# A decoder trunk in split precision on one core: first stage stepped by contraction tile, new orders on VectorE and ScalarE

## The reference

```python
def mixer_block(x, ...):
    h = rmsnorm(x, g_mix)
    za, zb, zc, zg = split(h @ w_in)
    ya = chunked_spatial_gating(gelu(za), ...) @ w_branch_a      # layernorm of v, masked 128x128 mix
    yb = short_gated_conv(zb, b_conv) @ w_branch_b
    yc = multiscale_pool(zc, c_wg, c_scale) @ w_branch_c
    gates = sigmoid(zg.reshape(nb, s, 3, D) + b_gate)
    return x + (gates[0] * ya + gates[1] * yb + gates[2] * yc) @ w_o

def cross_attention(x, mem, g_x, g_m, w_q, w_kv, w_o):           # 4 heads of 256
    q = rmsnorm(x, g_x) @ w_q
    k, v = split(rmsnorm(mem, g_m) @ w_kv)
    return x + softmax(q k^T * 256**-0.5) v @ w_o

def swiglu_ffn(x, g, w_in, w_out):                               # hidden 2816
    gate, up = split(rmsnorm(x, g) @ w_in)
    return x + (silu(gate) * up) @ w_out

# reference: mixer_block, cross_attention, swiglu_ffn, then rmsnorm(x, g_final)
```

## Time and profile before

| | us |
|---|---|
| median of 3 runs | 920.62 (920.34 to 920.63) |
| profiled execution | 920.04 |
| its span | 918.3 |
| TensorE busy | 900.6 (98%) |
| VectorE busy | 516.3 (56%) |
| ScalarE busy | 346.9 (38%) |
| mean granted TensorE clock | 0.995 |

### The profile page before, as it was taken

The page is one execution under the profiler, slowest core; times in us unless marked ns, Lnnn a source line. Parts: engine busy times, 40 slices in busy tenths (PEclk is TensorE's granted clock), DMA queues, the critical chain, the costliest instruction groups (busy, mean ns, idle before and its releaser), DMA issues.

```text
span 918.3 us, 12058 instructions
## 1 busy us (share of the span) xinstructions
PE 900.6 (98%) x4880; PEld 783.3 (85%) x4880; DVE 516.3 (56%) x600; ACT 346.9 (38%) x472; POOL 54.9 (6%) x59
## 2 busy tenths in 40 slices
PE   8999999999999999999999999989999999999997
PEld 6988888888888888888888888879999999888886
DVE  4576446683234245365456475988888887422333
ACT  5546322342222223232234332545545544323222
POOL 0101000000000000025100053000000000000000
PEclk9999999999999999999999999989999999999999
DMA  9842231322222222222121122222223223322212
GB/s 343 335 168 98 102 103 57 127 92 92 92 91 92 91 91 91 97 93 112 69 89 46 47 92 92 92 83 101 91 97 131 91 91 117 135 92 91 92 47 91
DMA packets 15040, 97.52 MB, mean 106 GB/s; under 512 B 1696, under 2 KB 1824, under 8 KB 4000
## 3 DMA queue, kind: packets, MB, share of 16 engines
q1 hardware_dynamic: 13968, 94.38, 28.3%
q0 software_dynamic: 464, 1.57, 0.6%
q10 hardware_dynamic: 576, 1.12, 0.4%
HBM read 94.97 MB, written 2.10 MB: 106 GB/s over the span
## 4 chain that ended last, share of the span: by engine, by line
PE 88%; DVE 6%; ACT 2%; DMA 1%; issue 1%; ACTq 0%; DVEq 0%; POOLq 0%; POOL 0%
PE psum L1253 29%; PE psum L1255 29%; PE psum L1254 29%; DVE wl L750 1%; DMA memr<-mem 1%; DVE tl L750 1%; DVE hn L1100 1%; DVE hl L753 0%; ACT th L368 0%; PE psum L1477 0%; PE psum L1303 0%; ACT pr L581 0%; PE psum L1601 0%; DVE xs L826 0%; DVE sm L1025 0%
## 5 line engine op out<-in xcount | busy, mean ns | idle before, releaser
L750 DVE TENSOR_TENSOR wl<-raw,wh 128x2048 fp32r<-128x2048 f32 (+1 forms) x56 | 116.8, 2094 | 145.3 <-ACT wh L368 145.2
L1253 PE MATMUL psum<-hh,wh 128*128 128x512 f32 x384 | 149.7, 390 | 0.0
L1255 PE MATMUL psum<-hh,wl 128*128 128x512 f32 x384 | 149.4, 389 | 0.0
L1254 PE MATMUL psum<-hl,wh 128*128 128x512 f32 x384 | 149.4, 389 | 0.0
L1253 PE MATMUL psum<-th,w7h 128*128 128x256 f32 x504 | 143.9, 285 | 5.0 <-DVE hid L1117 4.4
L1254 PE MATMUL psum<-tl,w7h 128*128 128x256 f32 x504 | 143.6, 285 | 0.0
L1255 PE MATMUL psum<-th,w7l 128*128 128x256 f32 x504 | 143.5, 285 | 0.0
L368 ACT ACTIVATE wh<-raw 128x2048 fp32r<-128x2048 f32 (+1 forms) x56 | 96.1, 1726 | 57.8 <-PE psum L1255 57.8
L1253 PEld LDWEIGHTS psum<-th,w7h 128*128 128x128 f32 x504 | 97.8, 194 | 5.7 <-DVE hid L1117 4.8
L1254 PEld LDWEIGHTS psum<-tl,w7h 128*128 128x128 f32 x504 | 97.8, 194 | 0.0
L1255 PEld LDWEIGHTS psum<-th,w7l 128*128 128x128 f32 x504 | 97.7, 194 | 0.0
(11 more groups left out here) (225 smaller groups left out, 1603.9 us busy)
## 6 DMA issues: line engine op xcount, KB each, us to landing
raw<-weights SPq DMA_DIRECT2D x79, 1024.0 KB, 4.8
vraw<-weights SPq DMA_DIRECT2D x3, 1024.0 KB, 13.7
xt<-xt SPq DMA_DIRECT2D x1, 2048.0 KB, 17.5
X<-x SPq DMA_DIRECT2D x2, 1024.0 KB, 28.2
out<-outb SPq DMA_DIRECT2D x8, 256.0 KB, 2.0
memt<-memt SPq DMA_DIRECT2D x1, 1024.0 KB, 23.4
vraw<-weights SPq DMA_DIRECT2D x2, 256.0 KB, 5.2
memr<-mem ACTq DMA_DIRECT2D x2, 256.0 KB, 7.9
```

Source lines behind the costliest of these rows:

```text
L750: return V.tensor_tensor(dst, v, f32(hi), ALU.subtract)
L1253: nc.tensor.matmul(dst, lh, rh, start=start, stop=False, **kw)
L1254: nc.tensor.matmul(dst, lh, rl, start=False, stop=False, **kw)
L1255: return nc.tensor.matmul(dst, ll, rh, start=False, stop=stop, **kw)
```

## The change

It touches six places.

1. Panels 0 and 1 of v land in pieces of 1, 1, 2, 2, 2 contraction tiles, and ScalarE and VectorE work in steps of one contraction tile: mem tile, then 512 columns of weights. The semaphores of the first eight steps are named by `of_piece`.
2. The warm-up products use `ones` alone, which POOL now writes first.
3. ScalarE and VectorE take the input's tiles in an order of their own ahead of and between the key panels.
4. The third normalization's column sums and spread stand inside tiles of the filler: ahead of contraction tile 6 of tile 0, and ahead of tile 4 of tile 1.
5. Filler 2's scaling stands between the last operand quarters, its silu ahead of the first block panel's rounding, its product behind the plain blocks. In the last seven-product panel the rounding of the weights and of `hid` are apart.
6. The tail: VectorE multiplies each half by g_final before the row factor is there; ScalarE applies the factor to the left half and issues its store.

```diff
-V_PIECES = ((0, 512), (512, 1024), (1024, 2048))
+V_PIECES = ((0, 1), (1, 2), (2, 4), (4, 6), (6, 8))
+        def of_piece(k, piece, panel):
+            return (panel, k // 4 + 1) if k % 4 == 3 else (piece, k + 1 - k // 4)
@@ gpsimd
+            nc.gpsimd.memset(ones[:], 1.0).then_inc(const_ready, 1)
             nc.gpsimd.memset(cst[:], -0.5).then_inc(const_ready, 1)
             chain(nc.gpsimd.memset(ident[:], 0.0))
-            nc.gpsimd.memset(ones[:], 1.0).then_inc(const_ready, 1)
@@ scalar
+            for k in range(KT):
+                for i, (a, b) in enumerate(MEM_PIECES):
+                    if k == a:
+                        act.wait_ge(mem_here[i], 16)
+                mem_hi(k)
+                for i, (a, b) in enumerate(V_PIECES):
+                    if k == a:
+                        act.wait_ge(v_piece[i], 16)
+                cs = slice(k % 4 * S, (k % 4 + 1) * S)
+                copy(wh[:, k // 4, cs], vraw[:, k // 4, cs]).then_inc(of_piece(k, piece_hi, hi_ready)[0], 1)
...
             h_hi(0)
+            h_hi(1)
             split_hi_halves(K0 + 2)
+            h_hi(2)
             k_hi(0)
-            h_hi(1)
+            h_hi(3)
             split_hi_halves(K0 + 3)
...
+            filler_silu(2)
             wh_blocks("plain", 0, FI0 + NF - 1, None)
             wh_blocks("s13", 0, None, 1)
             wh_blocks("s24", 0, None, 1)
             wh_blocks("corner", 0, None, None)
-            filler_silu(2)
...
-            act_window(NS - 1, 1, None, more=False, early=lambda: fo_hi(0))
+            act_window(NS - 1, 1, None, more=False, early=(lambda: fo_weights_hi(0), lambda: fo_hid_hi(0)))
...
+            def left_out(t):
+                act.wait_ge(f_rstd, t + 1)
+                act.wait_ge(f_gained, t + 1)
+                copy(outb[:, t, 0:S], outb[:, t, 0:S], scale=small(FR + t)).then_inc(f_left, 1)
+                act.wait_ge(f_left, t + 1)
+                act.dma_start(out[t * P:(t + 1) * P, 0:S], outb[:, t, 0:S]).then_inc(stored, 16)
...
+                    if half == 0 and t:
+                        left_out(t - 1)
+            left_out(TT - 1)
@@ vector
+            for k in range(KT):
+                mem_lo(k)
+                dve.wait_ge(*of_piece(k, piece_hi, hi_ready))
+                cs = slice(k % 4 * S, (k % 4 + 1) * S)
+                lo(wl[:, k // 4, cs], vraw[:, k // 4, cs], wh[:, k // 4, cs]).then_inc(of_piece(k, piece_lo, lo_ready)[0], 1)
...
             filler_product(1)
+            filler_scaled(2, 0)
             quarter_lo(5, high_banks)
+            filler_scaled(2, 1)
             dve.wait_ge(t_ready, 4)
             quarter_lo(6, low_banks)
...
             wl_plain(0, 0)
+            filler_product(2)
             wl_s13(0, 0)
-            filler_scaled(2, 0)
-            filler_scaled(2, 1)
             wl_s24(0, 0)
             wl_corner(0, 0)
-            filler_product(2)
...
+                left, right = bank[(4 + 2 * t) % 8], bank[(5 + 2 * t) % 8]
+                dve.wait_ge(f_sq, 2 * t + 1)
+                chain(V.tensor_scalar(small(FV + t), small(FS + 2 * t), 1.0 / D, EPS, ALU.mult, ALU.add))
+                V.tensor_tensor(outb[:, t, 0:S], left[:], gf[:, 0:S], ALU.mult).then_inc(f_gained, 1)
                 dve.wait_ge(f_sq, 2 * t + 2)
+                V.scalar_tensor_tensor(out=small(FV + t), in0=small(FS + 2 * t + 1), scalar=1.0 / D, in1=small(FV + t),
+                                       op0=ALU.mult, op1=ALU.add).then_inc(f_var, 1)
+                chain(V.tensor_tensor(outb[:, t, S:D], right[:], gf[:, S:D], ALU.mult))
                 dve.wait_ge(f_rstd, t + 1)
+                V.tensor_scalar(outb[:, t, S:D], outb[:, t, S:D], small(FR + t), None, ALU.mult).then_inc(f_out, 1)
@@ tensor
-            pe.wait_ge(const_ready, 3)
+            pe.wait_ge(const_ready, 1)
             for _ in range(WARM):
-                nc.tensor.matmul(bank[0][:, 0:P], ident[:], ones[:], start=True, stop=True)
+                nc.tensor.matmul(bank[0][:, 0:P], ones[:], ones[:], start=True, stop=True)
             v_half(0)
             v_half(1)
+            pe.wait_ge(const_ready, 3)
...
                     ins = fm_tile(bank[2 * (i % 2) + t], n % SLOTS, t, lambda k: hfh[:, k, :], lambda k: hfl[:, k, :],
-                                  ready=(hl_ready, 2 * KT) if i == 0 else None)
+                                  ready=(hl_ready, 2 * KT) if i == 0 else None,
+                                  between=((6, sum_x3), (4, spread_x3))[t] if i == 0 else None)
```

More of the change, by code:

```diff
@@ L200, in build @@
         mem_here = [sem(f"mem_here{i}") for i in range(3)]
-        v_piece = [sem(f"v_piece{i}") for i in range(3)]
-        v_panel = [sem(f"v_panel{i}") for i in range(4)]
+        v_piece = [sem(f"v_piece{i}") for i in range(5)]
+        v_panel = [sem(f"v_panel{i}") for i in range(2)]
         x_here = [sem(f"x_here{i}") for i in range(2)]
@@ L291, in _ @@
             for t in range(TT):
-                for half in range(2):
-                    sp.wait_ge(f_out, 2 * t + half + 1)
-                    cs = slice(half * S, (half + 1) * S)
-                    sp.dma_start(out[t * P:(t + 1) * P, cs], outb[:, t, cs]).then_inc(stored, 16)
+                sp.wait_ge(f_out, t + 1)
+                sp.dma_start(out[t * P:(t + 1) * P, S:D], outb[:, t, S:D]).then_inc(stored, 16)
             sp.wait_ge(stored, 16 * 2 * TT)
@@ L677, in act_window @@
                 if early:
-                    early()
+                    early[0]()
                 if more:
@@ L1255, in mm3, with fm_tile @@
                 return nc.tensor.matmul(dst, ll, rh, start=False, stop=stop, **kw)
-            def fm_tile(dst, slot, t, rh, rl, ks=range(KT), first=0, ready=None, free=None):
+            def fm_tile(dst, slot, t, rh, rl, ks=range(KT), first=0, ready=None, free=None, between=None):
                 for k in ks:
+                    if between and k == between[0]:
+                        between[1]()
                     if ready:
@@ L1315, in v_half @@
                         pe.wait_ge(meml_ready, k + 1)
-                    if half == 0 and k == 0:
-                        pe.wait_ge(piece_lo, 1)
-                    elif k % 4 == (1 if half == 0 and k < 4 else 0):
-                        pe.wait_ge(half_lo, n + 1)
+                        pe.wait_ge(*of_piece(k, piece_lo, lo_ready))
+                    elif k % 4 == 0:
+                        pe.wait_ge(half_lo, n - 1)
                     elif k % 4 == 2:
@@ L1527, in _, with sum_x3, spread_x3 @@
             out_part(3, range(8), True)
+            def sum_x3():
+                pe.wait_ge(res_acc, 2)
+                pe.wait_ge(exp_ready, TT * HEADS)
+                sum_columns(bank[4], acc2, TT).then_inc(res_sums, 1)
+            def spread_x3():
+                pe.wait_ge(res_rstd, 2)
+                spread(bank[4], GR, TT).then_inc(res_spread, 1)
             def filler(i):
```

112 lines of the change are left out of this document (37 added, 75 removed).

## The result

The changed kernel takes **911.34 us** (median of 4 runs, 911.21 to 911.57); the kernel before took 920.62 beside it (4 runs). The ratio is 0.9899, 95% interval 0.9882 to 0.9916. The profiled execution took 911.21 us, its span is 909.5 us; before, these were 920.04 and 918.3. The forecast was 910.2 us, range 908.6 to 912.6.

A forecast was written before the change was run, and what follows sets the result against it. TensorE was taken as the bound (88% of the chain), so gains lie only in its waits, slow clock and tail. 0.6 + 1.9 + 0 + 6.6 + 0.8 + 0.5 = 10.4 us gave 909.6 profiled, 910.2 us median, range 908.6 to 912.6.

The forecast's parts named there:

- Part 1: First stage: one-tile steps end half 0 1.5 us earlier, most given back; 0.6 us stays, bounds 0 and 1.5.
- Part 2: Keys and first v panel: the new x order removes two TensorE waits, 1.9 us, bounds 0.8 and 2.1.
- Part 5: Last seven-product panel: snapshots no longer behind the rounding of hid, idle gap goes, 0.8 us, bounds 0 and 0.8.
- Part 3: Third normalization: earlier sums and spread move VectorE's copy 2.8 us earlier; TensorE itself gains nothing.
- Part 4: Entry to seven-product panels: wait removed (4.5 us) and clock stays up (2.1 us), 6.6 us; bounds 4.5 and 6.8.
- what is next late: Second panel behind the entry: snapshot behind ScalarE's second rounding there at 605.5, wanted at 605.8, so no wait.
- Part 6: Tail: last square 0.45 us late, but shorter steps put both issues at 915.3, 0.5 us won; bounds -0.3 and 0.9.
- Lands later: Tail's worse bound, -0.3 us: the store issued on ScalarE's queue lands later than SP's.
- parts 1 to 3 would be eaten: Rival: landings of mem or x, or POOL's power beside the split, lose 0.6 + 0.5 + 0.8; 912.1, chance 0.14.
- The entry kept no wait: Rival at the seven-product entry: wait stays, 2.5 us idle, clock down, 4.1 of 6.6 lost; 914.5, chance 0.06.
- The slower case: Rival: VectorE's lag stays, each of 18 block windows waits 0.77 us; 3.5 us slower, 924.1, chance 0.03.
- The clock at the start: Rival: clock falls in longer idle before the first product, half speed some 4.7 us, 1.4 us later; 911.6, chance 0.10.

The follow-up runs named there:

- experiment 9: Changed kernel with the first stage stepped as in the kernel before, warm-up and later orders as changed: 912.12 us, ratio 0.9916.
- experiment 7: Changed kernel with the old order of the input's and keys' steps on VectorE and ScalarE: 913.41 us, ratio 0.9925.
- experiment 12: Changed kernel with the rounding of hid back ahead of the two snapshots in the last seven-product panel: 912.33 us, ratio 0.9919.
- experiment 3: Kernel before with only the entry's order changed (filler 2's scalings, silu and product at their new places): 916.42 us, ratio 0.9961.
- experiment 4: Changed kernel with the third normalization's column sums and spread back behind filler tiles 0 and 1: 912.76 us, ratio 0.992.
- experiment 5: Changed kernel, VectorE building all eight hn tiles before the low part of filler 2's weights and filler 0's first scaling: 909.88 us, ratio 0.9888.
- experiment 6: Changed kernel; VectorE scales both halves of the first three row tiles, ScalarE only the last one's left half, SyncE issues all stores: 911.30 us, ratio 0.9903.
- experiment 2: Changed kernel with the tail of before (combined multiplies on VectorE, all stores from SyncE's queue): 911.12 us, ratio 0.9903.
- experiment 11: Changed kernel; hn tiles ahead of filler 2's low part, fourth v panel's rounding behind three squares, ScalarE scaling only the last left half, SyncE storing: 908.54 us.
- experiment 10: Changed kernel; hn tiles ahead of filler 2's low part, and half the fourth v panel's rounding behind three of x's four squares: 909.98 us, ratio 0.9888.
- experiment 8: Changed kernel with 16 warm-up products instead of 24: 911.33 us, ratio 0.9909.

## Why the prediction was right, and where it was wrong

**Parts 1, 2 and 5** came as worked out, to 0.1 us each, and experiments 9, 7 and 12 give them one by one: 0.7, 1.9 (913.66 - 911.21 = 2.45 for the profiled executions, less the 0.53 by which that one came later to the keys) and 0.8. Inside part 1 two estimates missed and cancelled. I had the rest of mem landing at 14.33, as in the earlier trace rows, and a wait of 0.4 at tile 4. It lands at 12.76, and between 12.77 and 13.22 in all ten experiments with the new pieces, but at 14.54 and 14.60 with the old ones (3 and 9). SyncE now spends 3.04 us on issuing five pieces and asks for the third panel at 3.90 instead of 2.68; that this leaves the DMA engines to mem for longer is my reading, and no run isolates it. So the first half ended earlier than I said, and all of that was given back at panel 3, where x's landing (21.27, 21.33 before) sets the start: the gap was 1.27, not 0.9.

**Part 3** was put at nothing for TensorE with 2.8 us for VectorE's string; 2.7 was measured. That nothing was a matter of bookkeeping: experiment 4 shows 1.3 us of the gain at the entry hang on it.

**Part 4 is the step that was mis-sized**, 6.6 against 5.45. Its first half is right: the entry has no wait, the clock stays at 2.4 GHz, and TensorE gains 9.33 - 2.56 = 6.8 us by the 23rd product; the new wait takes back 1.32 with its restart. The step that failed is the opening one, that VectorE's string, 2.8 us earlier, is "still behind TensorE everywhere it must be". It shows in the sentence on "what is next late", by which the second panel's snapshot "is there at 605.5 and wanted at 605.8". It was wanted at 603.14, one step behind the product at 603.02, and done at 604.03 + 0.38 = 604.41: 1.6 us later than my 0.3 ahead of need.

My string on VectorE took over the idle times of before. But its earlier start brought it to filler 2's weights before ScalarE had rounded them: ScalarE may do so only when TensorE has multiplied filler panel 0, which shares the slot. In before the rounding was done at 566.64 + 1.92 = 568.56 and VectorE came at 570.85, 2.29 us of slack. In the changed kernel VectorE's string is 5.27 us earlier there, but the rounding only 1.63 (565.01), since part 3 itself put the spread inside the last tile of panel 0, ahead of its end (in experiment 4, with the spread behind that tile again, the rounding comes at 564.37, although that run is 0.30 us late). 5.27 - 1.63 - 2.29 = 1.35, and the row at 566.96 shows 1.30 us of idle time. This also took the entry's margin from 1.8 to 0.25 us. Experiment 5 moves this low part, with filler 0's scaling behind it, and the wait is gone.

**Part 6** is the other miss, 0.5 against 0.0. The small steps are shorter as forecast, and only one pass of 0.5 to 0.7 us stands behind the power. The square was 0.35 us late (0.78 behind the last product, 0.43 before), near the 0.45 that I had. What failed is the count to the last issue: I had the second store of the last row tile 0.5 us earlier and took it that the end moves with it. SyncE's issues of that tile in before, in the changed kernel and in experiment 6:

```profile
915.18 0.99 SPq L295 DMA_DIRECT2D out<-outb  x2
```

```profile
906.39 0.33 SPq L298 DMA_DIRECT2D out<-outb  x1
```

```profile
906.36 0.81 SPq L300 DMA_DIRECT2D out<-outb  x2
```

The first store is issued 2.93, 2.91 and 2.55 us behind the last product (912.25, 903.48, 903.81), and the span ends 3.1, 3.1 and 3.0 us behind that issue. The second store does come sooner in the changed kernel, 0.16 us behind the first instead of 0.6, but then it lands in 2.5 us instead of 2.0. The landings of this tile's two stores, first in the changed kernel, then in experiment 6, where SyncE issues both, 0.35 us apart:

```profile
DMA to landing us min/median/max: 2.0/2.3/2.5
```

```profile
DMA to landing us min/median/max: 2.0/2.2/2.3
```

So in these traces the tail is as long as the string up to the first store, and in the changed kernel the late square took back what the shorter steps won there. "Lands later" was the worse bound of this part, and I named it without weighing it; that it would be ScalarE's queue as such isn't borne out, since SyncE's own second store lands later too when it follows closely. Experiment 2, with the tail of before, issues its first store 2.93 us behind the last product and agrees that the whole is worth nothing. Experiments 6 and 11 take the late square away, and are 0.4 us shorter from the last product on.

**The sum.** 10.4 - 8.83 = 1.6 us were not there: 1.15 at the entry, 0.45 in the tail. The median made up for some: I set it 0.58 over the profiled execution, as before, and it was only 0.13 over. That part of the hit is luck. The lower end of the range was added up wrongly, too: the better bounds of parts 1 and 6 are 0.9 and 0.4 us better, which gives 908.9 and not 908.6; and 4.1 us lost at the entry is 914.3, not 914.5. Neither bears on the result.

**The rivals.** That parts 1 to 3 would be eaten did not come; POOL's power took 3.00 us again, beside the same split. The entry kept no wait, but by a margin that makes this rival's 0.06 too small: with the hidden tile 1.3 us later (experiment 4) it waits 0.98. The slower case stayed away: behind the first window no window waits, and VectorE had idle time in each, 1.22 us for the silu and 0.27 for TensorE in most.

**The clock at the start** is the rival that needs mending. In the changed kernel's own profile the warm-up products took 7.89 us, not the 7.2 that I moved up from the earlier trace rows, so the idle time ahead of the first product was 1.12 us and nothing fell. But the fall is real. Of the 12 experiments' profiled executions three show it: 4, 7 and 10, with 2.21, 2.24 and 1.95 us of idle time. Eight with 0.67 to 1.47 us, or with no idle time noted, do not, and neither does experiment 8 with 3.17. My price of 1.4 us was wrong for this kernel. From the first product to the first key product, experiments 4 and 7 take 24.26 and 24.28 us, against 24.13: the clock was down from about 11 to 14 us, not for the 4.7 us that I took from the entry, the slow products only fill the gap ahead of panel 3, and the cost is 0.15 us. Once experiments 10 and 11 shrink that gap, the same fall costs 24.31 - 23.22 = 1.1 us. That is why experiment 10's median hides what its edit wins. The single long runs of experiments 8 (1.5 us) and 11 (1.7 us) may be of this kind. For experiment 11 the mean granted clock on record speaks for it (0.997, the others 0.998 and 0.999). Experiment 8's kernel has the gap ahead of panel 3, where such a fall should cost 0.15 us and not 1.5, so its long run stays open.

## What to carry to other kernels

When a string of work moves earlier, its idle times don't move with it: ask of each step what it waits for, and whether that has moved too, and whether the edit itself puts work ahead of it, as the spread inside the filler's tile did here. A place where another engine's landing sets the restart absorbs losses ahead of it as well as gains, so an edit that removes it makes the kernel faster and also more sensitive. Read terms of under 1 us from fixed points of two traces, and look at the clock of the first microseconds before taking a median as the verdict on an edit.

## What the runs showed of the hardware

- The same 48 warm-up records (24 products of two passes) took between 6.98 and 8.47 us in different executions, with a granted clock of 1.00 in all their windows. At first 6 or 7 of them ran in a microsecond, later 11 or 12. The faster pace began at 4 to 4.6 us from the span's start in the three executions whose clock then fell to 1.2 GHz 0.5 to 0.9 us behind the first real product (experiments 4, 7 and 10), and at 5 to 7 us in all others, those of the kernel before and of experiment 8 (32 records) with them, whose clock stayed up. Whether the late change of pace and the clock that stays up have one cause, no run isolates.
- Idle time doesn't bring the fall by its length alone: after the entry's wait in the kernel before it fell in the third microsecond, 1.95 us of idle time were enough in experiment 10, and 3.17 us in experiment 8 brought no fall.
- Two 256 KB stores issued close together: the first landed in 2.0 us, the second in 2.0 when it was issued 0.64 us behind the first (kernel before, both SyncE's), in 2.3 at 0.35 us (experiment 6, both SyncE's), in 2.2 at 0.5 and in 2.5 at 0.16 us (changed kernel, the second ScalarE's). The second was down 2.6 to 2.7 us behind the first one's issue each time, from either queue.
